# A two-layer trunk step: PSUM columns in one run over two banks, and taps of the up convolution read from PSUM

## The chip, the cores and the metric

The kernel runs on one core of one Trainium2 chip. The metric is the device time of one execution in microseconds, the median of three executions. One profiled execution, with a time of its own, gives the trace from which every row below is copied.

## What is computed

A trunk of two layers works on 128 prompt tokens and 512 sample tokens with 1024 channels. Each layer has a token-mixing half (attention, a convolution, a spatial gating and a pooling branch, gated and merged) and a gated feed-forward half. The second half, which the change touches most, is

```
def conv_ffn(h, lp):
    up = depthwise_conv(h @ lp['ffn_up'], lp['ffn_dw'], lp['ffn_dw_b'])
    gate, val = up[..., :D_FF], up[..., D_FF:]
    return (jax.nn.silu(gate) * val) @ lp['ffn_down']
```

with `D_FF = 2816` and a convolution of three taps along the tokens, padded with zeros at both ends of each group. All of it is float32 at the inputs and outputs.

## The kernel before, in words

**Layout.** Channels lie on the 128 partitions and tokens along the free dimension. A line has `TOK = 644` columns: 128 prompt tokens, two zero columns, 512 sample tokens, two zero columns. PSUM has eight banks of 512 float32 columns. The kernel uses them as four sets (0 to 3) of two banks, and a tile of 644 columns lies in a set as two halves of `HALF = 322`, one in each bank.

**Products.** Each large product is made in three float32r passes: the weights and the activations are both split in a high and a low part, and `hi*hi`, `lo*hi` and `hi*lo` are summed in PSUM (`product`, `first_group`, `down_chunk`). GpSimd splits the weights (`w_raw` into `w_hi` and `w_lo`, L435 and L437), 128x512 at a time, in a ring of four slots. So one output tile and one chunk of 128 input channels is three passes of two matmuls of 322 columns: three pairs. In a layer come the input projection (p1, 16 tiles), attention, the merge (`merge`, 8 steps), the output projection (`out`, 8 tiles), and then `up` (44 tiles of 8 chunks) and `down` (8 tiles of 22 chunks). Between the products stand RMS norms, in which TensorE does little.

**The up stage.** Its 44 tiles go in 11 steps of four, tile j of a step in PSUM set j. A step makes two pairs q: tiles 0 and 1 (gate and value of one chunk of 128 channels) and tiles 2 and 3. The first step is `first_group`, which runs over the input chunks outside and the tiles inside; the others run tile after tile. For each tile ScalarE (ACT) copies the 644 columns from PSUM into `up_x` in SBUF (L1157) and then gives the set free (L1159). For each pair VectorE (DVE) makes the middle tap with the bias out of `up_x` (L1666, two instructions), then the two outer taps (L1671, four instructions) into `up_y`; ScalarE takes the tanh (L1164); VectorE makes the gate and the product (L1678, L1681) into `act`.

**The ada work.** In steps 1 to 8 VectorE also sums three tiles of the modulation weights (`ada`, L1258 and L1260: 16 instructions of 384 columns) ahead of the pairs of that step. TensorE adds these sums over the partitions with twelve small matmuls (L528; six in the program, each of which stands in the trace as two) before tile 3 of the same step, into columns of tile 3's own set, and ScalarE keeps the result ahead of its copy of tile 3. So in a step TensorE waits before tile 3 for VectorE's sums; VectorE waits for tile 3 to be complete before pair 1, and the next sums stand behind pair 1 on its engine.

**The down stage.** Each chunk of `act` is split by ScalarE (`hi_part`, L1175) and VectorE (`lo_part`, L1688) and multiplied into all four sets (`down_chunk`, L838).

What sets the order is the order of the code on each engine, with counting semaphores between the engines: `set_full` and `set_empty` for the PSUM sets, `w_split` and `w_used` for the ring, `up_copied`, `up_conv`, `up_tanh`, `act_ready`.

Of the kernel before, what the change touches and what calls it, by code (L numbers as in the profile page):

```python
# [56 lines left out]
HALF = TOK // 2  # L57
# [81 lines left out]
EDGE = 8  # L139
# [7 lines left out]
def trunk_kernel(nc, x_in, cond_in, w_ada, w_lin, w_merge, w_pair, params_in, tables_in, ctx_ckv, ctx_kpe, const_in,  # L147
                 y_out, ckv_out, kpe_out):
    with ExitStack() as ctx:
# [95 lines left out]
        up_x = u("up_x", 0, 4 * 648, shape=[4, 648])  # L245
# [12 lines left out]
        def halves(s, lo=0, hi=P):  # L258

            return ps[lo:hi, 2 * s:2 * s + 2, 0:HALF]  # L260

# [7 lines left out]

        def two(ap):  # L270
            return ap.rearrange("p (a b) -> p a b", a=2)
# [203 lines left out]
        def _(pe):  # L475
# [4 lines left out]
            def product(L, phase, r, s, blocks, rhs, k_wait=None):  # L480
# [22 lines left out]
            def first_group(L, phase, rhs, k_wait):  # L503


                for k in range(DC):
# [4 lines left out]
                    for s in range(4):  # L511
                        whi, wlo = w_hi[:, k % SLOTS, s * P:(s + 1) * P], w_lo[:, k % SLOTS, s * P:(s + 1) * P]
                        for i, (w, a) in enumerate(((whi, hi), (whi, lo), (wlo, hi))):
                            for j in range(2):
                                last = pe.matmul(ps[:, 2 * s + j, 0:HALF], w, a[:, j * HALF:(j + 1) * HALF],  # L515
                                                 start=(k == 0 and i == 0), stop=(k == DC - 1 and i == 2))
# [5 lines left out]
            def ada(n, s):  # L522

                pe.wait_ge(ada_summed, n)
                for t in range(ADA_TRIO):
                    for g in range(2):
                        at = HALF + 2 * t + g
                        pe.matmul(ps[:, 2 * s, at:at + 1], ada_part[:, g, t, :], ones[:, 0:1], start=True, stop=True)  # L528
# [59 lines left out]
            with pe.Fori(0, DEPTH) as L:  # L588
# [154 lines left out]
                for c in range(2):  # L743
# [3 lines left out]
                    for j in range(2):  # L747
                        last = pe.matmul(ps[:, 2 * (2 + c) + j, 0:HALF], w, br[:, 8 + c, j * HALF:(j + 1) * HALF], start=True, stop=True)
# [78 lines left out]
                def down_chunk(pass_, chunk, nth, slot, par_, start, stop):  # L827
# [3 lines left out]
                    for s in range(4):  # L831
# [4 lines left out]
                        for i, (w, a) in enumerate(((whi, hi), (whi, lo), (wlo, hi))):  # L836
                            for j in range(2):
                                last = pe.matmul(ps[:, 2 * s + j, 0:HALF], w, a[:, j * HALF:(j + 1) * HALF],  # L838
                                                 start=(start and i == 0), stop=(stop and i == 2))
# [19 lines left out]
        def _(ac):  # L859
# [49 lines left out]
            def keep_ada(s, dst, t=0, n=ADA_TRIO):  # L909

                at = HALF + 2 * t
                return ac.activation(dst.rearrange("p a b -> p (a b)"), ps[:, 2 * s, at:at + 2 * n], ACT.Copy)
# [11 lines left out]
            with ac.Fori(0, DEPTH) as L:  # L924
# [41 lines left out]
                for c in range(2):  # L966
# [9 lines left out]
                    p0, in_first = 2 * EDGE + SEQ, HALF - SAMPLE0  # L976
# [894 lines left out]
```

## Time and profile before

| | us |
|---|---|
| median of three executions | 2735.32 (2733.73 to 2735.55) |
| the profiled execution | 2733.34 |
| its span in the trace | 2731.5 |
| TensorE matmul busy in it | 2473.2 |
| TensorE weight load busy | 2303.1 |
| VectorE busy | 1636.3 |
| ScalarE busy | 536.3 |
| GpSimd busy | 1303.7 |
| mean granted TensorE clock | 0.936 of 2.4 GHz |

Busy time of an engine is the union of its instructions. A matmul is drawn from its start until its result is through, and successive matmuls overlap, so the price of one in a stream is read from the distance of two starts, not from its duration. A "<-" in brackets names what ended an idle time.

### The profile page before, as it was taken

The page shows a single profiled execution, that of the slowest core. Times are in us where ns is not written, and L with a number is a line of the kernel's source. Part 1 is how long each engine was busy: PE and PEld are TensorE (multiplying, and loading weights), DVE is VectorE, ACT ScalarE, POOL GpSimd, SP SyncE. Part 2 cuts the span into 40 slices and gives each one's busy share as a digit, 9 for nine tenths or more (in the row PEclk, how much of TensorE's full clock was granted, in tenths as well). Part 3 has the DMA queues.
Part 4 walks back from the last instruction along what each step waited for, and adds up shares of the span by engine and source line. Part 5 has one row for each costly group of instructions (what it writes and reads, how often), then busy time and mean ns, then how long its engine had stood idle before and what let it go on. Part 6 is the DMA issues. An engine that isn't in the chain of part 4 may idle for free.

```text
span 2731.5 us, 44570 instructions
## 1 busy us (share of the span) xinstructions
PE 2473.2 (91%) x15092; PEld 2303.1 (84%) x15092; DVE 1636.3 (60%) x2288; ACT 536.3 (20%) x917; POOL 1303.7 (48%) x1232
## 2 busy tenths in 40 slices
PE   7897889999978999999969888899999789999996
PEld 7894449999977998899969745699999688889995
DVE  4558756444347777765473786644451677776655
ACT  1203432110022111112221144311011211111221
POOL 1458304555534544465525761165555244445552
PEclk9998989999978999999969989999999799999998
DMA  5110103333312333222212101133332133332221
GB/s 209 57 53 13 40 8 103 117 117 97 95 43 74 104 106 102 81 72 73 66 30 85 34 10 38 39 121 117 94 114 79 28 105 104 104 103 68 72 70 58
DMA packets 100479, 211.92 MB, mean 78 GB/s; under 512 B 10208, under 2 KB 17824, under 8 KB 100384
## 3 DMA queue, kind: packets, MB, share of 16 engines
q1 hardware_dynamic: 84832, 151.66, 18.9%
q10 hardware_dynamic: 15552, 59.02, 6.0%
q8 instruction: 57, 0.93, 0.1%
q14 instruction: 38, 0.31, 0.0%
HBM read 207.71 MB, written 2.93 MB: 77 GB/s over the span
## 4 chain that ended last, share of the span: by engine, by line
PE 68%; DVE 12%; DVEq 11%; ACT 3%; issue 3%; DMA 1%; ACTq 1%; SPq 0%
PE ps L495 37%; PE ps L838 10%; PE ps L515 6%; DVEq L1263 4%; DVE ada_part L1260 4%; PE ps L713 3%; PE ps L565 3%; DVEq L1668 2%; PE ps L528 2%; PE ps L659 1%; DVEq L1674 1%; DVEq L1529 1%; PE ps L689 1%; PE ps L702 1%; PE ps L579 1%
## 5 line engine op out<-in xcount | busy, mean ns | idle before, releaser
L435 POOL TENSOR_SCALAR w_hi<-w_raw 128x512 fp32r<-128x512 f32 x552 | 371.8, 674 | 1222.0 <-PE ps L495 296.4
L437 POOL TENSOR_TENSOR w_lo<-w_raw,w_hi 128x512 fp32r<-128x512 f32 x552 | 758.7, 1374 | 81.4 <-issue 1.2
L495 PE MATMUL ps<-h_hi,w_hi 128*128 128x322 f32 x2688 | 636.5, 319 | 0.0
L495 PE MATMUL ps<-h_lo,w_hi 128*128 128x322 f32 x2688 | 631.9, 317 | 0.0
L495 PE MATMUL ps<-h_hi,w_lo 128*128 128x322 f32 x2688 | 627.8, 315 | 0.0
L495 PEld LDWEIGHTS ps<-h_lo,w_hi 128*128 128x128 f32 x2688 | 466.9, 194 | 0.0
L495 PEld LDWEIGHTS ps<-h_hi,w_hi 128*128 128x128 f32 x2688 | 465.2, 194 | 1.3 <-issue 1.3
L495 PEld LDWEIGHTS ps<-h_hi,w_lo 128*128 128x128 f32 x2688 | 466.1, 194 | 0.0
L1260 DVE SCALAR_TENSOR_TENSOR ada_part<-ada_raw,cond,ada_part 128x384 f32<-128x384 f32 x448 | 341.5, 803 | 19.3 <-issue 3.4
L1688 DVE TENSOR_TENSOR a_lo<-act,a_hi 128x644 fp32r<-128x644 f32 x88 | 135.3, 1541 | 148.6 <-ACT a_hi L1175 147.6
L1671 DVE SCALAR_TENSOR_TENSOR up_y<-up_x,par,up_y 128x644 f32<-128x644 f32 x176 | 179.3, 1060 | 13.2 <-issue 11.3
L838 PE MATMUL ps<-a_hi,w_hi 128*128 128x322 f32 x704 | 162.8, 313 | 6.7 <-DVE a_lo L1688 6.7
L838 PE MATMUL ps<-a_hi,w_lo 128*128 128x322 f32 x704 | 163.1, 313 | 0.0
L838 PE MATMUL ps<-a_lo,w_hi 128*128 128x322 f32 x704 | 162.8, 312 | 0.0
L1617 DVE SCALAR_TENSOR_TENSOR mtmp<-gate_t,ps 128x644 f32<-128x644 f32 x48 | 39.4, 821 | 173.0 <-ACT gate_t L1106 114.7
L1666 DVE TENSOR_SCALAR up_y<-up_x,par 128x644 f32<-128x644 f32 x88 | 65.1, 782 | 123.1 <-ACT up_x L1157 123.1
L838 PEld LDWEIGHTS ps<-a_hi,w_hi 128*128 128x128 f32 x704 | 119.6, 191 | 8.0 <-DVE a_lo L1688 7.8
L838 PEld LDWEIGHTS ps<-a_hi,w_lo 128*128 128x128 f32 x704 | 119.6, 191 | 0.0
L838 PEld LDWEIGHTS ps<-a_lo,w_hi 128*128 128x128 f32 x704 | 119.5, 191 | 0.0
L1106 ACT ACTIVATE gate_t<-ps,half_gate 128x644 f32<-128x644 f32 x64 | 51.3, 801 | 340.6 <-PE ps L495 337.2
L1223 DVE TENSOR_TENSOR sq_sum<-sq_sum,sq 128x644 f32<-128x644 f32 x38 | 39.3, 1035 | 128.5 <-ACT sq L867 127.0
L1164 ACT ACTIVATE up_t<-up_y 128x644 f32<-128x644 f32 x44 | 32.7, 744 | 414.3 <-DVE up_y L1671 414.3
(200 smaller groups left out, 3492.4 us busy)
## 6 DMA issues: line engine op xcount, KB each, us to landing
w_raw<-in_w_lin_dram SPq DMA_DIRECT2D x360, 256.0 KB, 2.6
ada_raw<-in_w_ada_dram ACTq DMA_DIRECT2D x32, 1536.0 KB, 6.7
w_raw<-in_w_merge_dram SPq DMA_DIRECT2D x144, 256.0 KB, 2.7
ada_pre<-in_w_ada_dram ACTq DMA_DIRECT2D x4, 2048.0 KB, 21.8
w_raw<-in_w_merge_dram SPq DMA_DIRECT2D x48, 128.0 KB, 2.0
pw<-in_w_pair_dram SPq DMA_DIRECT2D x8, 640.0 KB, 3.9
x<-in_x_dram SPq DMA_DIRECT2D x8, 322.0 KB, 6.0
out_y_dram<-x SPq DMA_DIRECT2D x8, 322.0 KB, 2.3
```

The costliest lines, as they stand in the source:

```text
L435: pool.tensor_scalar(w_hi[:, s, 0:n * P], raw, 1.0, 0.0, ALU.mult, ALU.add)
L437: pool.tensor_tensor(w_lo[:, s, 0:n * P], raw, w_hi[:, s, 0:n * P], ALU.subtract).then_inc(w_split[s], 1)
L495: last = pe.matmul(ps[:, 2 * s + j, 0:HALF], w, a[:, j * HALF:(j + 1) * HALF], start=(k == 0 and i == 0), stop=(k == total - 1 and i == 2))
L515: last = pe.matmul(ps[:, 2 * s + j, 0:HALF], w, a[:, j * HALF:(j + 1) * HALF], start=(k == 0 and i == 0), stop=(k == DC - 1 and i == 2))
L565: last = pe.matmul(ps[:, 6, b:b + 1], sq[:, c % 2, BLOCK_COL[b]:BLOCK_COL[b] + P], ones[:, 0:1], start=False, stop=(c == DC - 1 and b == N ...
L713: pe.matmul(ps[0:V_HEAD, 7, :], v_pair[:, b, vs], probs_t[:, b, :], start=(b == 0), stop=(b == 4))
L838: last = pe.matmul(ps[:, 2 * s + j, 0:HALF], w, a[:, j * HALF:(j + 1) * HALF], start=(start and i == 0), stop=(stop and i == 2))
L1260: last = dv.scalar_tensor_tensor(out=acc[:, g, 0:n, :], in0=w, scalar=cond[:, k, g:g + 1], in1=acc[:, g, 0:n, :], op0=ALU.mult, op1=ALU.add)
L1263: dv.drain()
L1666: dv.tensor_scalar(up_y[:, j, :], up_x[:, j, 2:2 + TOK], col("ffn_dw", v, 1), col("ffn_dw_b", v), ALU.mult, ALU.add)
L1671: last = dv.scalar_tensor_tensor(out=up_y[:, j, :], in0=up_x[:, j, 1 + tap:1 + tap + TOK], scalar=col("ffn_dw", v, tap), in1=up_y[:, j, :] ...
L1688: dv.tensor_tensor(a_lo[:, n % 2, :], src, a_hi[:, n % 2, :], ALU.subtract).then_inc(a_ready, 1)
```

## The change

The 644 columns of a tile lie in one run: columns 0 to 511 fill the first bank of the set, columns 512 to 643 the first 132 columns of the second. Each pass of a product is now three matmuls, of 256, 256 and 132 columns. The first opens the accumulation in the first bank, the second ends it; the third does both in the second bank. The ada columns move behind column 132 of the second bank. Every reader of a tile takes 644 columns in one run instead of two halves, at the same count; only the pooling input needs one copy less (2 for 3 of them, four times in all).

In the up stage ScalarE's copy to `up_x` becomes the middle tap itself: an activation `Identity` with the tap as scale and the bias, out of PSUM into `up_y`. VectorE's two instructions of the middle tap are gone; its four outer taps read 643 columns straight from PSUM, where neighbouring tokens lie side by side. The set is given free by VectorE after its taps and no longer by ScalarE after its copy. `up_x` and its zeroed edges are gone, and ScalarE's middle tap waits for `act_ready` of the step before, since `up_y` is written earlier.

```
-HALF = TOK // 2
+BANK = 512
+REST = TOK - BANK
+PARTS = ((0, 0, 256, True, False), (0, 256, 256, False, True), (1, 0, REST, True, True))
...
         def halves(s, lo=0, hi=P):
 
-            return ps[lo:hi, 2 * s:2 * s + 2, 0:HALF]
+            return line(s, TOK, lo, hi)
...
+        def par_col(name, i, j, tap=0):
+
+            at = PCOL[name] + tap * 2 * FFC + j
+            return par[:, i * 4 + at:i * 4 + at + 1] if isinstance(i, int) else par[:, bass.ds(i * 4 + at, 1)]
...
                         for i, (w, a) in enumerate(((whi, hi), (whi, lo), (wlo, hi))):
-                            for j in range(2):
-                                last = pe.matmul(ps[:, 2 * s + j, 0:HALF], w, a[:, j * HALF:(j + 1) * HALF],
-                                                 start=(k == 0 and i == 0), stop=(k == total - 1 and i == 2))
+                            for bank, at, m, opens, ends in PARTS:
+                                col = bank * BANK + at
+                                last = pe.matmul(ps[:, 2 * s + bank, at:at + m], w, a[:, col:col + m],
+                                                 start=(k == 0 and i == 0 and opens), stop=(k == total - 1 and i == 2 and ends))
...
-                        if j % 2 == 0:
-
-                            ac.wait_ge(up_conv, L * FFC + (q + 1) + i * 2)
-                        ac.activation(two(up_x[:, j, 2:2 + TOK]), halves(j), ACT.Copy).then_inc(up_copied, 1)
-                        ac.wait_ge(up_copied, L * (2 * FFC) + (j + 1) + i * 4)
-                        ac.sem_inc(set_empty[j], 1)
+                        if j % 2 == 0 and not first:
+
+                            ac.wait_ge(act_ready, L * FFC + q + i * 2 - 1)
+                        ac.activation(up_y[:, j, :], halves(j), ACT.Identity, scale=par_col("ffn_dw", i, j, 1), bias=par_col("ffn_dw_b", i, j))\
+                            .then_inc(up_copied, 1)
...
                         dv.wait_ge(up_copied, L * (2 * FFC) + (2 * q + 2) + i * 4)
-                        for v in range(2):
-                            j = 2 * q + v
-                            dv.tensor_scalar(up_y[:, j, :], up_x[:, j, 2:2 + TOK], col("ffn_dw", v, 1), col("ffn_dw_b", v), ALU.mult, ALU.add)
-                        for tap in (0, 2):
-                            dv.drain()
+                        for tap, of, to in ((0, 0, 1), (2, 1, 0)):
                             for v in range(2):
                                 j = 2 * q + v
-                                last = dv.scalar_tensor_tensor(out=up_y[:, j, :], in0=up_x[:, j, 1 + tap:1 + tap + TOK], scalar=col("ffn_dw", v, tap),
-                                                               in1=up_y[:, j, :], op0=ALU.mult, op1=ALU.add)
+                                dst = up_y[:, j, to:to + TOK - 1]
+                                last = dv.scalar_tensor_tensor(out=dst, in0=line(j, TOK)[:, of:of + TOK - 1], scalar=par_col("ffn_dw", i, j, tap),
+                                                               in1=dst, op0=ALU.mult, op1=ALU.add)
+                            if tap == 0:
+                                dv.drain()
                         last.then_inc(up_conv, 1)
                         dv.drain()
+                        for v in range(2):
+                            dv.sem_inc(set_empty[2 * q + v], 1)
```

`first_group` and `down_chunk` get the same `PARTS` loop as `product`.

On TensorE, in the loop over steps 1 to 8 of the up stage, at the ada matmuls and the start of tile 3 (`ps` is PSUM, `h_hi` and `h_lo` the activations, `w_hi` and `w_lo` the weights), before:

```order
1197 L816 REGISTER_ALU
1198 L524 REGISTER_ALU
1199 L528 MATMUL ps<-const,ada_part 128x1 x6
1200 L495 MATMUL ps<-h_hi,w_hi 128x322 x2
1201 L495 MATMUL ps<-h_lo,w_hi 128x322 x2
1202 L495 MATMUL ps<-h_hi,w_lo 128x322 x2
```

and with the change:

```order
2069 L824 REGISTER_ALU
2070 L532 REGISTER_ALU
2071 L536 MATMUL ps<-const,ada_part 128x1 x6
2072 L502 MATMUL ps<-h_hi,w_hi 128x256 x2
2073 L502 MATMUL ps<-h_hi,w_hi 128x132
2074 L502 MATMUL ps<-h_lo,w_hi 128x256 x2
2075 L502 MATMUL ps<-h_lo,w_hi 128x132
2076 L502 MATMUL ps<-h_hi,w_lo 128x256 x2
2077 L502 MATMUL ps<-h_hi,w_lo 128x132
```

Each pass of two matmuls has become one of three; nothing else moved there. On ScalarE, in the same loop, from tile 0 to tile 2, before:

```order
412 L1156 ISA [waits set_full0]
413 L1157 ACTIVATE up_x<-ps 128x644 [waits up_conv]
414 L1158 ISA
415 L1140 REGISTER_ALU [waits up_copied]
416 L1157 ACTIVATE up_x<-ps 128x644 [waits set_full1]
417 L1158 REGISTER_ALU
418 L1163 REGISTER_ALU [waits up_copied]
419 L1164 ACTIVATE up_t<-up_y 128x644 [waits up_conv]
420 L1140 REGISTER_ALU
421 L1156 REGISTER_ALU [waits set_full2]
422 L1157 ACTIVATE up_x<-ps 128x644 [waits up_conv]
```

and with the change:

```order
400 L1164 ISA [waits set_full0]
401 L1165 ISA [waits act_ready]
402 L1165 REGISTER_ALU
403 L1165 ACTIVATE up_y<-ps,par 128x644
404 L1148 REGISTER_ALU
405 L1165 ISA [waits set_full1]
406 L1165 ACTIVATE up_y<-ps,par 128x644
407 L1170 REGISTER_ALU
408 L1171 ACTIVATE up_t<-up_y 128x644 [waits up_conv]
409 L1148 REGISTER_ALU
410 L1164 REGISTER_ALU [waits set_full2]
411 L1165 ISA [waits act_ready]
```

The activation out of PSUM stays, with the tap and the bias from `par`; its wait for `up_copied` and the release behind it are gone, and `act_ready` stands where `up_conv` stood. On VectorE, one pair of a step without ada work, before:

```order
607 L1666 TENSOR_SCALAR up_y<-up_x,par 128x644 [waits up_copied]
608 L1666 TENSOR_SCALAR up_y<-up_x,par 128x644
609 L1671 SCALAR_TENSOR_TENSOR up_y<-up_x,par,up_y 128x644 x4
610 L1677 REGISTER_ALU
611 L1678 SCALAR_TENSOR_TENSOR up_t<-up_t,up_y 128x644 [waits up_tanh]
612 L1681 SCALAR_TENSOR_TENSOR act<-up_t,up_y 128x644
```

and with the change:

```order
589 L1667 SCALAR_TENSOR_TENSOR up_y<-ps,par,up_y 128x643 [waits up_copied]
590 L1667 SCALAR_TENSOR_TENSOR up_y<-ps,par,up_y 128x643 x3
591 L1677 REGISTER_ALU
592 L1678 SCALAR_TENSOR_TENSOR up_t<-up_t,up_y 128x644 [waits up_tanh]
593 L1681 SCALAR_TENSOR_TENSOR act<-up_t,up_y 128x644
```

The two instructions of the middle tap are gone and the four outer taps read `ps` instead of `up_x`.

## Rows read from the trace of the kernel before

**Rows 1.** The page, part 1: busy us (share of the span) xinstructions.

```profile
PE 2473.2 (91%) x15092; PEld 2303.1 (84%) x15092; DVE 1636.3 (60%) x2288; ACT 536.3 (20%) x917; POOL 1303.7 (48%) x1232
```

**Rows 2.** Groups on PE, shapes apart: xcount | busy us, mean ns | idle before.

```profile
L495 PE MATMUL ps<-h_hi,w_hi 128*128 128x322 f32 x2688 | 636.5, 319 | 0.0
L838 PE MATMUL ps<-a_hi,w_hi 128*128 128x322 f32 x704 | 162.8, 313 | 6.7 <-DVE a_lo L1688 6.7
...
L495 PE MATMUL ps<-br_hi,w_hi 128*128 128x322 f32 x320 | 73.3, 310 | 0.0
...
L515 PE MATMUL ps<-h_hi,w_hi 128*128 128x322 f32 x256 | 62.9, 329 | 16.0 <-DVE h_lo L1325 16.0
...
L515 PE MATMUL ps<-mg_hi,w_hi 128*128 128x322 f32 x128 | 29.8, 314 | 2.4 <-DVE mtmp L1617 2.4
...
L495 PE MATMUL ps<-mg_hi,w_hi 128*128 128x322 f32 x128 | 29.5, 312 | 0.0
...
L641 PE MATMUL ps<-ws_t,tok_major 128*64 128x128 f32 x80 | 4.8, 275 | 3.7 <-DVEq L1480 3.7
```

**Rows 3.** Timeline of PE in p1 of the second layer: start us, us, what, xcount.

```profile
1480.24 0.46 PE L495 MATMUL ps<-h_hi,w_hi 128*128 128x322 f32 x2
...
1489.77 0.46 PE L495 MATMUL ps<-h_hi,w_lo 128*128 128x322 f32 x2
```

**Rows 4.** Windows: us, PE busy (x), PEld, DVE, ACT, POOL, PEclk, DMA share, GB/s.

```profile
1300.00:1360.00 60.00, 60.00 (x406) 60.00 (x405) 26.95 (x17) 12.66 (x17) 33.09 (x32) 1.00 0.26 75
```

**Rows 5.** Timeline of the weight loads, attention's matmuls of 512, 256 and 128 columns.

```profile
216.80 0.19 PEld L668 LDWEIGHTS ps<-ckv,pw 128*128 128x128 f32 x1 [0.24 <-issue]
217.23 0.62 PEld L668 LDWEIGHTS ps<-ckv,pw 128*128 128x128 f32 x3 [0.24 <-issue]
217.88 2.86 PEld L676 LDWEIGHTS ps<-pw,ckv 128*128 128x128 f32 x24
```

**Rows 6.** Timeline of the weight loads: ada matmuls of one column, then 322.

```profile
443.87 1.42 PEld L528 LDWEIGHTS ps<-const,ada_part 128*128 128x128 f32 x12 [1.01 <-DVE ada_part L1260]
445.20 0.30 PEld L495 LDWEIGHTS ps<-h_hi,w_hi 128*128 128x128 f32 x2
```

**Rows 7.** Windows of the up stage: layer 0, one step of it, layer 1.

```profile
878.00:1136.50 258.50, 227.76 (x1431) 225.61 (x1429) 202.30 (x237) 29.25 (x50) 125.53 (x115) 0.92 0.32 102
...
920.40:955.30 34.90, 31.74 (x206) 31.47 (x205) 27.72 (x33) 4.17 (x7) 17.68 (x16) 0.95 0.31 105
...
2212.40:2471.00 258.60, 227.90 (x1431) 225.75 (x1429) 202.28 (x237) 29.24 (x50) 125.53 (x115) 0.92 0.32 102
```

**Rows 8.** Timeline of PE: the waits for the ada sums in layer 0.

```profile
886.98 2.72 PE L528 MATMUL ps<-const,ada_part 128*128 128x1 f32 x12 [8.67 <-DVE ada_part L1260]
...
958.79 2.05 PE L528 MATMUL ps<-const,ada_part 128*128 128x1 f32 x12 [3.16 <-DVE ada_part L1260]
```

**Rows 9.** Timeline of DVE, one step: pair 1, then the next ada sums.

```profile
935.95 1.37 DVE L1666 TENSOR_SCALAR up_y<-up_x,par 128x644 f32<-128x644 f32 x2 [3.84 <-ACT up_x L1157]
937.50 2.04 DVE L1671 SCALAR_TENSOR_TENSOR up_y<-up_x,par,up_y 128x644 f32<-128x644 f32 x2 [0.18 <-issue]
...
958.66 0.61 DVE L1666 TENSOR_SCALAR up_y<-up_x,par 128x644 f32<-128x644 f32 x1
```

**Rows 10.** Groups on DVE with a PSUM operand or of the up stage.

```profile
L1671 DVE SCALAR_TENSOR_TENSOR up_y<-up_x,par,up_y 128x644 f32<-128x644 f32 x176 | 179.3, 1060 | 13.2 <-issue 11.3
...
L1617 DVE SCALAR_TENSOR_TENSOR mtmp<-gate_t,ps 128x644 f32<-128x644 f32 x48 | 39.4, 821 | 173.0 <-ACT gate_t L1106 114.7 <-PE ps L495 57.6 <-issue 0.8
```

**Rows 11.** Timelines at the end of the first up step: DVE, PE.

```profile
855.89 1.14 DVE L1666 TENSOR_SCALAR up_y<-up_x,par 128x644 f32<-128x644 f32 x2 [11.59 <-ACT up_x L1157]
...
856.66 0.46 PE L495 MATMUL ps<-h_hi,w_hi 128*128 128x322 f32 x2
```

**Rows 12.** Timelines at the start of the down stage: ACT, PE.

```profile
1205.80 0.71 ACT L1157 ACTIVATE up_x<-ps 128x644 f32<-128x644 f32 x1 [3.82 <-PE ps L495]
...
1214.65 0.57 PE L838 MATMUL ps<-a_hi,w_hi 128*128 128x322 f32 x2 [1.85 <-DVE a_lo L1688]
```

More of the change, by code:

```diff
@@ L513, in first_group @@
                         for i, (w, a) in enumerate(((whi, hi), (whi, lo), (wlo, hi))):
-                            for j in range(2):
-                                last = pe.matmul(ps[:, 2 * s + j, 0:HALF], w, a[:, j * HALF:(j + 1) * HALF],
-                                                 start=(k == 0 and i == 0), stop=(k == DC - 1 and i == 2))
+                            for bank, at, m, opens, ends in PARTS:
+                                col = bank * BANK + at
+                                last = pe.matmul(ps[:, 2 * s + bank, at:at + m], w, a[:, col:col + m],
+                                                 start=(k == 0 and i == 0 and opens), stop=(k == DC - 1 and i == 2 and ends))
                         if k == DC - 1:
@@ L526, in ada @@
                     for g in range(2):
-                        at = HALF + 2 * t + g
-                        pe.matmul(ps[:, 2 * s, at:at + 1], ada_part[:, g, t, :], ones[:, 0:1], start=True, stop=True)
+                        at = REST + 2 * t + g
+                        pe.matmul(ps[:, 2 * s + 1, at:at + 1], ada_part[:, g, t, :], ones[:, 0:1], start=True, stop=True)
             def two_blocks(j):
@@ L746, in _ @@
                     w = tables[:, 768 + c * P:768 + (c + 1) * P]
-                    for j in range(2):
-                        last = pe.matmul(ps[:, 2 * (2 + c) + j, 0:HALF], w, br[:, 8 + c, j * HALF:(j + 1) * HALF], start=True, stop=True)
+                    for bank, n in ((0, BANK), (1, REST)):
+                        last = pe.matmul(ps[:, 2 * (2 + c) + bank, 0:n], w, br[:, 8 + c, bank * BANK:bank * BANK + n], start=True, stop=True)
                     last.then_inc(set_full[2 + c], 1)
@@ L836, in down_chunk @@
                         for i, (w, a) in enumerate(((whi, hi), (whi, lo), (wlo, hi))):
-                            for j in range(2):
-                                last = pe.matmul(ps[:, 2 * s + j, 0:HALF], w, a[:, j * HALF:(j + 1) * HALF],
-                                                 start=(start and i == 0), stop=(stop and i == 2))
+                            for bank, at, m, opens, ends in PARTS:
+                                col = bank * BANK + at
+                                last = pe.matmul(ps[:, 2 * s + bank, at:at + m], w, a[:, col:col + m],
+                                                 start=(start and i == 0 and opens), stop=(stop and i == 2 and ends))
                         if stop:
@@ L909, in keep_ada @@
             def keep_ada(s, dst, t=0, n=ADA_TRIO):
-                at = HALF + 2 * t
-                return ac.activation(dst.rearrange("p a b -> p (a b)"), ps[:, 2 * s, at:at + 2 * n], ACT.Copy)
+                at = REST + 2 * t
+                return ac.activation(dst.rearrange("p a b -> p (a b)"), ps[:, 2 * s + 1, at:at + 2 * n], ACT.Copy)
             for i in range(ADA_LOADS):
@@ L975, in _ @@
                     ac.wait_ge(pool_x_free, L * 3 + (c + 1))
[L976 removed]
+                    p0 = 2 * EDGE + SEQ
                     ac.activation(pool_x[:, EDGE:EDGE + SEQ], ps[:, 2 * s, 0:SEQ], ACT.Copy)
[L978 to L979 removed]
+                    ac.activation(pool_x[:, p0:p0 + DEC_SEQ], line(s, TOK)[:, SAMPLE0:SAMPLE0 + DEC_SEQ], ACT.Copy)\
                         .then_inc(set_empty[s], 1)
@@ L1645, in _ @@
                 next_h(L, "gap2", L * 2 + 1, L * NINV + 3, mods(L, ADA_TRIOS), MOD_FFN, ADA, "pre_ffn_g")
-                for j in range(4):
-                    dv.memset(up_x[:, j, 0:2], 0.0)
-                    dv.memset(up_x[:, j, 2 + TOK:4 + TOK], 0.0)
-                dv.drain()
                 def up_step(i, last_step=False, with_ada=False):
@@ L1655, in up_step @@
                     for q in range(2):
-                        def col(name, v, tap=0):
-                            at = PCOL[name] + tap * 2 * FFC + 2 * q + v
-                            return par[:, i * 4 + at:i * 4 + at + 1] if isinstance(i, int) else par[:, bass.ds(i * 4 + at, 1)]
                         if last_step and q == 1:
```

9 lines of the change are left out of this document (2 added, 7 removed).

## The prediction

> **What bounds the kernel now.** I read the engines' busy shares first: TensorE's matmuls fill 91% of the span and VectorE 60% [rows 1]. Then TensorE's groups: six groups of float32r matmuls of 322 columns, with 2688, 704, 320, 256, 128 and 128 instructions, and each has two companions of the same count for the other passes [rows 2]. That is 3 x 4224 = 12,672 matmuls, or 6336 pairs, and their idle time before is small. In p1 two rows that stand 32 rows (64 matmuls) apart start 9.53 us apart, so one matmul costs 148.9 ns and a pair 297.8 ns [rows 3]; a window of the down stage agrees, 406 in 60 us without a gap, at the full clock of 2.4 GHz [rows 4]. 6336 x 0.2978 = 1887 us: the kernel is for two thirds of its time a stream of these pairs.
>
> One place is different, the up stage with ada work. From the first wait for the sums to the end of the eighth it takes 258.5 us in layer 0 and 258.6 in layer 1, seven steps plus one wait [rows 7]. TensorE waits there 8.67 us once and then 3.16 us in each step for VectorE's ada sums [rows 8], and the mean clock is 0.92, because after each wait it is granted 1.2 GHz for a while. Its own work at full clock is 96 pairs and twelve one-column matmuls, 28.6 + 1.3 = 29.9 us, against steps of 34.9 us [rows 7]. So here VectorE's and TensorE's hand-over bounds.
>
> **The change, part by part.**
>
> *Three matmuls for two.* Each pass keeps its 644 columns but loads its weights three times instead of twice: 6336 more matmuls and weight loads. What does one cost? The 148.9 ns of 322 columns are 134.2 ns of columns at 2.4 GHz and 14.7 ns more. For 256 columns that gives 118.4 ns if the surplus goes with the columns and 121.4 ns if it is fixed. For 132 columns the columns alone would be 61 ns, but the next weights must be loaded meanwhile. Twelve matmuls of one column, which have nothing but their loads to do, take 1.33 us until the next, 111 ns each, and the first float32r load behind them, drawn with its successor as 0.30 us of which the last load is 0.19, also takes 0.11 us [rows 5, 6]. So the 132-column part costs a weight load, 111 ns. The triple is 2 x 118.4 + 111 = 348 or 2 x 121.4 + 111 = 354 ns; I take **351 ns**, 53.2 ns over a pair. From below it can't be under three weight loads, 3 x 111 = 333 ns. From above a 256-column part can't cost more than a 322-column one, 2 x 148.9 + 111 = 409; but the float32 rows of attention go with their columns, 0.43 us for 512, (0.62 - 0.19)/2 = 0.215 for 256 and (2.86 - 0.19)/23 = 0.116 for 128 at two cycles a column [rows 5], so I put the working upper end at three times the fixed surplus, 3 x 121.4 = 364 ns, and leave more to a rival.
>
> The Trainium skill, TensorE: Matmul & The Clock Gate, section LDWEIGHTS (loading the stationary operand), gives a load of 128 columns as 128/1.2, 107 ns, so it too says that a 132-column matmul doesn't hide the next load; the trace has 111. The same page's section Back-to-back issue gap has a rule against this: N/2.4 + 2.5 ns for a lone matmul, 109 + 109 + 57.5 = 276 ns for a triple. By that rule a pair would be 273 ns, where the trace has 298.
>
> *Where this lies on the path.* Of the 6336 pairs 2 x 7 x 96 = 1344 lie in the two stretches of the up stage above. The other 4992 run where TensorE waits for next to nothing: 4992 x 0.0532 = **+265.6 us**. Only a wait before the spatial gating's matmuls, 3.7 us in all for VectorE [rows 2], is filled by the longer stream: **-3.7 us**.
>
> *The up stage with ada.* TensorE's step becomes 96 x 0.351 + 1.33 = 35.0 us. VectorE's cycle before was: sums ready at 923.8 (the next are ready at 958.66, one step of 34.9 later), then ada matmuls, tile 3 and ScalarE's copy until 935.95, then 1.55 us for the middle tap, then 21.16 us for the outer taps, the gate and the next sums [rows 7, 9]. The middle tap leaves VectorE (ScalarE's activation stays as one of 0.7 us); tile 3 grows by 24 x 0.0532 = 1.3 us. That is 12.15 + 1.3 + 21.16 = 34.6 us, and some 2 us less once tile 3 is no longer run at the half clock. Both are under 35.0: TensorE becomes the bound, its waits of 8.67 and 3.16 us go, and with them the half clock. Seven steps: 245.2 us for 258.5, **-26.7 us** over both layers. With 333 ns the step is 33.3 and with 364 ns 36.3 us, -51 and -9 us.
>
> *Taps from PSUM.* An instruction of the same kind with one PSUM operand takes 821 ns in the merge, where those of `up_x` take 1060 on average [rows 10]. I leave this gain at nothing: VectorE is hidden behind TensorE now. It would be worth something only if VectorE bounded again.
>
> *Sets given free later.* ScalarE released a set after its copy; VectorE now does after the taps of the pair. In a running step this is hidden: pair 0's taps, some 3.5 us, start when the sums are ready, and TensorE then has the ada matmuls and tile 3, 9.8 us, before it wants set 0. It shows twice in a layer. After `first_group` all four tiles end together: VectorE starts at 855.89 and TensorE goes on at 856.66 [rows 11]; the taps now end 3.5 us after such a start, so TensorE waits about 2.6 us. What is late next is nothing: its ada sums are then ready before tile 3. At the start of the down stage sets 2 and 3 come free about 4.8 us after the last up tile, where TensorE wants set 2 after 2.1 us: 2.6 us, of which the present wait of 1.85 us for `a_lo` two chunks later [rows 12] is given back. 2 x (2.6 + 0.7) = **+6.6 us**. Bounds: 0 if the waits overlap others, 12 if the next wait stays. The ada columns' new place, the pooling copy and the dropped zeroing cost nothing I can see; ScalarE, 20% busy, covers them.
>
> *The sum.* 2733.3 (the profiled execution) + 265.6 - 3.7 - 26.7 + 6.6 = 2975.1. The median of the runs is 2.0 above the profiled one: **2977 us**, 8.8% slower.
>
> **The rivals.**
>
> A. *A short float32r matmul costs more than its columns or its load.* No row shows one under 322 columns. If the 132-column part fell to the float32 price (attention's matmuls of 128 columns are two records of 111 ns each), it would cost 223: the triple is 461 ns, the 4992 pairs 815 us, and seven steps of 45.6 us 319 us for 258.5, +121: about 3675. If every float32r matmul cost 149 ns whatever its width (a price per instruction), the triple is 447 ns: 745 + 101 us, about 3585. For it: the surplus of 14.7 ns over the columns is unexplained, where the float32 matmuls have 2 to 5. Against it: one load behind one-column matmuls took 0.11 us [rows 6], and float32 matmuls, issued just like these, go at 111.
>
> B. *Faster: the loads hide.* If the second and third load of the same weights cost nothing and only columns count, a triple stays at 298 ns and only the up stage moves: VectorE's cycle, with tile 3 at 7.1 us and full clock, is 8.5 + 1.8 + 21.2 = 31.5 us (1.8 is an estimate for the copy of 0.7 [rows 12] with its hand-overs), 220 us for 258.5 in each layer, -76: 2733.3 - 76 + 6.6 + 2 = 2666. The point from which it decides: with the stage still bound by VectorE, at (76 - 7)/4992 = 14 ns more for a triple, or 312 ns, gain and loss are even. Against it: today both halves load the same weights and each load is there, 15,092 for 15,092 matmuls [rows 1], and one-column matmuls still take 111 ns. By the skill's lone-matmul rule above the estimate would be 4992 x -0.022 more, about 2556.
>
> C. *VectorE stays the bound in the up stage.* If the taps from PSUM took 1.7 us each instead of 0.8 (VectorE and TensorE on PSUM at once), its cycle gains 4 x 0.8 us and is 36 us: +14 us, 2991. For it: nothing in the trace reads PSUM at such a rate beside matmuls; against it the merge's 821 ns, taken beside a full TensorE [rows 10].
>
> That the change doesn't do what it says is out: the order of the changed kernel has the three matmuls.
>
> **How the numbers follow.** Forecast 0.78, A 0.12, B 0.05, C 0.05. With the bounds of the triple: 333 ns gives 2733 + 176 - 51 + 5 = 2863, 364 ns gives 2733 + 330 - 9 + 5 = 3059; the uncertain waits add 6. I give **2870 to 3070**, since the lower end needs every surplus gone; C lies inside, A and B outside with 0.17. Faster by over 0.2% (about what a measurement of this kernel can tell from no change): 0.04, B. Within 0.2%: 0.01. Slower: 0.95.
>
> **What would show it.** In the changed trace: 19,008 float32r matmuls; starts 118 to 121 ns apart for the 256s and 111 from the 132 to the next; eight merge steps longer by 126 x 53 ns = 6.7 us each; in the up stage no wait before the ada matmuls, steps of 35.0 us and a full clock; TensorE waits of 2 to 3 us after `first_group` of `up` and at the start of `down`, for VectorE. A is shown by starts of over 140 ns behind the short part, B by ones near 61. I am wrong as a whole if TensorE stays below the full clock in a stream that is load-bound for a third of its matmuls.

## The result, and the profile after

| | before | after |
|---|---|---|
| median of the runs beside each other, us | 2734.53 (2732.31 to 2735.55) | 2943.53 (2940.08 to 2944.98) |
| ratio, 95% interval | | 1.0764 [1.0745, 1.0782] |
| the profiled execution, us | 2733.34 | 2940.08 |
| its span, us | 2731.5 | 2938.3 |
| mean granted TensorE clock | 0.936 | 0.958 |

The changed kernel is 7.6% slower: 206.7 us between the two profiled executions, where the prediction's sum had 241.8. One of the 13 executions of the kernel before that were timed beside the run of 322s with the copy (below) took 4735 us at a granted clock of 1.0; it stands in no ratio here. The engines' busy times and the chain that ended last, from the page of after (the first line answers to [rows 1]):

```profile
PE 2742.8 (93%) x21428; PEld 2581.0 (88%) x21428; DVE 1520.9 (52%) x2184; ACT 554.0 (19%) x913; POOL 1265.9 (43%) x1232
...
PE 87%; DVE 5%; DVEq 2%; ACT 2%; issue 2%; DMA 1%; ACTq 0%; SPq 0%
```

TensorE has 21428 - 15092 = 6336 matmuls more and holds 87% of the chain that ended last; in the same line of the page of before it was 68%, with 12% for VectorE and 11% for its sequencer. The kernel has become more purely a TensorE kernel, at a better clock, and slower.

Groups of after, shapes apart (columns as in [rows 2]; the VectorE line answers to [rows 10]):

```profile
L502 PE MATMUL ps<-h_hi,w_hi 128*128 128x256 f32 x2688 | 605.1, 306 | 5.1 <-DVEq L1672 5.1
...
L502 PE MATMUL ps<-h_hi,w_hi 128*128 128x132 f32 x1344 | 302.7, 225 | 0.0
...
L847 PE MATMUL ps<-a_hi,w_hi 128*128 128x256 f32 x704 | 157.8, 306 | 5.5 <-DVEq L1672 5.0 <-DVE a_lo L1688 0.5
...
L649 PE MATMUL ps<-ws_t,tok_major 128*64 128x128 f32 x80 | 4.8, 275 | 0.0
```

```profile
L1667 DVE SCALAR_TENSOR_TENSOR up_y<-ps,par,up_y 128x643 f32<-128x643 f32 x176 | 147.8, 881 | 247.0 <-ACT up_y L1165 240.7 <-issue 5.4
```

The only new waits of TensorE are those for `L1672`, the release of the sets behind VectorE's taps: once in `up` and once in `down` in each layer, 2.5 us each. The wait of 3.7 us before the spatial gating is gone. A tap out of PSUM takes 881 ns, one out of `up_x` took 1060.

The stream itself, in p1 of the second layer, three matmuls a row (answers to [rows 3]):

```profile
1553.50 0.51 PE L523 MATMUL ps<-h_hi,w_lo 128*128 128x256 f32 x3
...
1559.41 0.51 PE L502 MATMUL ps<-h_lo,w_hi 128*128 128x256 f32 x3
```

The second row stands 17 rows below the first (where `first_group`, L523, has given way to `product`, L502), 5.91 us later: a pass of 256 + 256 + 132 takes 347.6 ns. The 216 passes between the eighth ada matmuls and `down` agree: 75.09 us, 347.6 ns each. The pair of before took 297.8.

Windows of after: a piece of the down stage, the up stage from the first ada matmul to the eighth in layer 0 and in layer 1, and from the end of `first_group` to the first ada matmul (columns as in [rows 4]; the middle two answer to [rows 7] without its first wait):

```profile
1400.00:1460.00 60.00, 60.00 (x521) 60.00 (x520) 24.29 (x14) 10.40 (x14) 28.13 (x29) 1.00 0.21 62
...
966.40:1209.30 242.90, 242.90 (x2103) 242.90 (x2102) 164.20 (x196) 35.46 (x50) 114.03 (x112) 1.00 0.33 106
...
2403.50:2646.30 242.80, 242.80 (x2102) 242.80 (x2101) 164.26 (x196) 35.35 (x50) 114.00 (x112) 1.00 0.33 106
...
937.30:966.40 29.10, 26.57 (x216) 26.58 (x217) 26.20 (x31) 5.05 (x7) 13.09 (x12) 0.94 0.33 108
```

In the up stage TensorE has no gap in 242.9 us, at the full clock: seven steps of 34.7 us. Before, the same seven steps took 249.5 us; with the wait ahead of them they are the 258.5 us of [rows 7], at a clock of 0.92. The three starts that matter, in the timeline of TensorE of after (the first answers to [rows 11], the second to [rows 8], the third to [rows 12]):

```profile
939.83 0.56 PE L502 MATMUL ps<-h_hi,w_hi 128*128 128x256 f32 x3 [2.53 <-DVEq L1672]
...
966.45 1.45 PE L536 MATMUL ps<-const,ada_part 128*128 128x1 f32 x12
...
1290.45 0.56 PE L847 MATMUL ps<-a_hi,w_hi 128*128 128x256 f32 x3 [2.50 <-DVEq L1672]
```

The ada matmuls no longer wait; the two new waits stand where sets are wanted that VectorE has just read.

Where the 206.7 us came from, by stages (us, from the start of the first matmul of each):

| stage | before, layer 0 / 1 | after | difference | predicted, each layer |
|---|---|---|---|---|
| p1 | 128.3 / 127.1 | 144.3 / 144.2 | +16.0 / +17.1 | +18.6 |
| attention | 205.3 / 207.3 | 204.1 / 204.0 | -1.2 / -3.3 | 0 |
| merge | 312.7 / 312.5 | 362.3 / 362.3 | +49.6 / +49.8 | +53.6 |
| out | 59.4 / 59.4 | 69.0 / 69.0 | +9.6 / +9.6 | +10.2 |
| up to its first ada matmul | 60.6 / 60.6 | 65.4 / 65.4 | +4.8 / +4.8 | -1.8 with the next |
| first to eighth ada matmul | 249.5 / 249.6 | 242.9 / 242.9 | -6.6 / -6.7 | |
| eighth ada matmul to down | 69.0 / 69.0 | 76.4 / 76.4 | +7.4 / +7.4 | +11.5 |
| down | 165.6 / 165.2 | 189.1 / 189.0 | +23.5 / +23.8 | +28.8 |

The last column is the prediction's sum spread over the stages: 384, 1008, 192, 168 + 672, 216 and 528 passes in a layer, with its waits and, for the up stage, its seven steps. The norms inside the layers are the same to 0.1 us; the norm between the layers takes 0.6 us more, the start 0.7 and the tail 0.2.

### The profile page after: what moved, and what is told of

It is laid out like the page before. It is cut to its first block, busy times and chain, and to the rows that moved or that the text cites. A ratio compares the mean times of both kernels' runs of the same rounds, so it can differ in the third digit from the quotient of the medians.

```text
span 2938.3 us, 56947 instructions
## 1 busy us (share of the span) xinstructions
PE 2742.8 (93%) x21428; PEld 2581.0 (88%) x21428; DVE 1520.9 (52%) x2184; ACT 554.0 (19%) x913; POOL 1265.9 (43%) x1232
## 4 chain that ended last, share of the span: by engine, by line
PE 87%; DVE 5%; DVEq 2%; ACT 2%; issue 2%; DMA 1%; ACTq 0%; SPq 0%
PE ps L502 56%; PE ps L847 12%; PE ps L523 7%; PE ps L721 3%; PE ps L573 2%; PE ps L536 1%; PE ps L667 1%; DVEq L1535 1%; PE ps L697 1%; PE ps L710 1%; PE ps L587 1%; DMA ada_pre<-in_w_ada_dram 1%; ACT probs L1021 1%; DVE conv_acc L1550 1%; PE ps L684 1%
## 5 line engine op out<-in xcount | busy, mean ns | idle before, releaser
L502 PE MATMUL ps<-h_hi,w_hi 128*128 128x256 f32 (+1 forms) x4032 | 688.6, 279 | 5.1 <-DVEq L1672 5.1
L502 PE MATMUL ps<-h_hi,w_lo 128*128 128x256 f32 (+1 forms) x4032 | 687.0, 279 | 0.0
L502 PE MATMUL ps<-h_lo,w_hi 128*128 128x256 f32 (+1 forms) x4032 | 686.5, 279 | 0.0
L502 PEld LDWEIGHTS ps<-h_hi,w_hi 128*128 128x128 f32 x4032 | 561.8, 189 | 6.7 <-issue 6.7
L502 PEld LDWEIGHTS ps<-h_lo,w_hi 128*128 128x128 f32 x4032 | 562.7, 190 | 0.0
L502 PEld LDWEIGHTS ps<-h_hi,w_lo 128*128 128x128 f32 x4032 | 562.3, 189 | 0.0
L1267 DVE SCALAR_TENSOR_TENSOR ada_part<-ada_raw,cond,ada_part 128x384 f32<-128x384 f32 x448 | 346.6, 814 | 17.1
L1667 DVE SCALAR_TENSOR_TENSOR up_y<-ps,par,up_y 128x643 f32<-128x643 f32 x176 | 147.8, 881 | 247.0 <-ACT up_y L1165 240.7
L847 PE MATMUL ps<-a_hi,w_hi 128*128 128x256 f32 (+1 forms) x1056 | 179.5, 278 | 5.5 <-DVEq L1672 5.0
L847 PE MATMUL ps<-a_hi,w_lo 128*128 128x256 f32 (+1 forms) x1056 | 179.6, 278 | 0.0
L847 PE MATMUL ps<-a_lo,w_hi 128*128 128x256 f32 (+1 forms) x1056 | 178.9, 277 | 0.0
```

Of the source, the lines that this page charges most:

```text
L502: last = pe.matmul(ps[:, 2 * s + bank, at:at + m], w, a[:, col:col + m], start=(k == 0 and i == 0 and opens), stop=(k == total - 1 and i = ...
L847: last = pe.matmul(ps[:, 2 * s + bank, at:at + m], w, a[:, col:col + m], start=(start and i == 0 and opens), stop=(stop and i == 2 and ends))
L1267: last = dv.scalar_tensor_tensor(out=acc[:, g, 0:n, :], in0=w, scalar=cond[:, k, g:g + 1], in1=acc[:, g, 0:n, :], op0=ALU.mult, op1=ALU.add)
L1667: last = dv.scalar_tensor_tensor(out=dst, in0=line(j, TOK)[:, of:of + TOK - 1], scalar=par_col("ffn_dw", i, j, tap), in1=dst, op0=ALU.mult ...
```

## The experiments

Theory: a float32r matmul costs its columns or one weight load of 111 ns, whichever is longer, and a pass is the sum of its parts. The taps read from PSUM free TensorE from its waits in the up stage. Rivals: each matmul has a price of its own whatever its width; repeated loads of the same weights are free; the layout (a run over two banks) costs something in its readers.

In the kernels below the changed kernel's parts come from two numbers, with the matmul loops otherwise as they are: `START`, the first column of the run in its set, and the sizes of the parts. Every reader takes the run from `START` on.

**The load for itself: two parts, 512 and 132.**

```
-PARTS: 256, 256, 132 from column 0
+PARTS: 512, 132 from column 0
```

> The changed kernel with two matmuls a pass instead of three: 512 columns fill the first bank, 132 the second. Theory (a part costs its columns at 0.462 ns each or the next weight load of 111 ns, whichever is longer): 512 x 0.462 + 111 = 348 ns for 644 columns, as in the changed kernel, so its time stays at 2935 to 2950 us although a third of the matmuls is gone. Rival 1 (the third matmul costs some 50 ns as an instruction): the pass falls back to 298 ns and the kernel to about 2680 us. Rival 2 (each load adds its share to the columns it lies beside): two loads instead of three give about 315 ns, some 2780 us.

Measured: 2914.59 us (2913.61 to 2919.46), ratio 1.0667 [1.0649, 1.0685]. Timeline of TensorE in p1, two matmuls a row:

```profile
1544.83 0.51 PE L508 MATMUL ps<-h_hi,w_hi 128*128 128x512 f32 x2
...
1551.69 0.50 PE L508 MATMUL ps<-h_hi,w_lo 128*128 128x512 f32 x2
```

Twenty rows, 6.86 us: 343 ns a pass. With as many matmuls and loads as before (15,092), the kernel is 6.7% slower, since one part of the two is under a load's time; the kernel of the next experiment, which differs from it in the two sizes and the first column alone, is 253 us faster. So it isn't the number of instructions: what costs is a part too short to cover the load of the next weights. The measured time lies 20 us below the theory's range. The 512-column matmul must then be 343 - 111 = 232 ns, 18.7 over its 213.3 of columns, where the theory had let the surplus grow with the columns.

**The taps alone: 322 and 322, in one run.**

```
-PARTS: 256, 256, 132 from column 0
+PARTS: 322, 322 from column 190
```

> The changed kernel with the run of 644 columns begun at column 190 of a set, so that 322 columns lie in each bank and a pass is two matmuls of 322 again; taps from PSUM stay. It is the second part of the change alone. Theory: TensorE's stream is that of before (298 ns a pair), and in the up stage VectorE bounds with a step of 31.5 to 33 us for 35.6, with waits of some 2.7 us at two places of each layer: 2665 to 2700 us, faster than both kernels. Rival (reading the taps from PSUM or giving the sets free later costs something in each step): 2735 us or more.

Measured: 2661.72 us (2659.44 to 2663.43), ratio 0.9738 [0.9722, 0.9755]: the only kernel here that beats both, by 72 us under before and 282 under after, and 3 us below the expected range. The window from the first to the eighth ada matmul, then one wait of TensorE for the sums, then VectorE's taps, in layer 0:

```profile
887.00:1106.30 219.30, 214.63 (x1429) 212.76 (x1429) 168.16 (x197) 35.74 (x50) 118.27 (x112) 0.98 0.36 118
...
917.86 1.50 PE L541 MATMUL ps<-const,ada_part 128*128 128x1 f32 x12 [0.67 <-DVE ada_part L1271]
...
930.47 1.68 DVE L1671 SCALAR_TENSOR_TENSOR up_y<-ps,par,up_y 128x643 f32<-128x643 f32 x2 [5.75 <-ACT up_y L1169]
```

31.3 us a step, where before has 35.6 between these two marks; rival B had worked out 31.5 from VectorE's cycle. The wait for the sums shrinks from 3.16 us [rows 8] to 0.67, and the clock rises from 0.92 to 0.98. The seven steps of both layers give 60.7 us, the pieces of the up stage before and behind them another 13.9. p1, merge, out and the norms don't move.

**The triple alone: parts as in the changed kernel, the up stage with its copy.**

The copy's waits and `up_x` with its zeroed edges come back too; of the edit this is the core (`...` marks cuts, within lines too):

```
-ac.activation(up_y[:, j, :], halves(j), ACT.Identity, scale=..., bias=...)
+ac.activation(two(up_x[:, j, 2:2 + TOK]), halves(j), ACT.Copy)
+ac.sem_inc(set_empty[j], 1)
...
+dv.tensor_scalar(up_y[:, j, :], up_x[:, j, 2:2 + TOK], ...)   # middle tap, two of them
-in0=line(j, TOK)[:, of:of + TOK - 1]                           # outer taps
+in0=up_x[:, j, 1 + tap:1 + tap + TOK]
```

> The first part of the change alone: one run over two banks in parts of 256, 256 and 132, but ScalarE copies to SBUF, VectorE makes all three taps from there and ScalarE gives the set free, as before. Theory: the stream costs 348 ns a pass, +250 us, and in the up stage TensorE's 34.7 us and VectorE's 34 to 35.5 us nearly tie, so the taps' part is worth little under the triple: 2945 to 2965 us. Rival (the later release costs more than the taps save): under 2940 us.

Measured: 2961.09 us (2959.01 to 2961.74), ratio 1.0832 [1.0814, 1.085]. The same seven steps, and one start of the ada matmuls:

```profile
965.90:1218.30 252.40, 251.30 (x2101) 250.25 (x2101) 197.75 (x225) 29.25 (x50) 124.19 (x112) 0.97 0.30 101
...
965.93 2.72 PE L537 MATMUL ps<-const,ada_part 128*128 128x1 f32 x12 [4.78 <-DVE ada_part L1269]
```

252.4 us against the 242.9 with the taps from PSUM. The longer stream alone already fills most of the waits: the first one, ahead of this window, is 4.78 us for 8.67, and within it TensorE is idle for 1.1 us. What stays is the clock of 0.97.

**The layout alone: 322 and 322 in one run, with the copy.** This kernel has the parts of `e2` and the up stage of `e3`.

> The kernel before with nothing changed but the layout: the 644 columns lie in one run over the two banks, begun at column 190, in two matmuls of 322; ScalarE copies to SBUF and VectorE takes its taps from there. Theory (a run over two banks costs and gives nothing by itself; all that the run of 322s with taps from PSUM gained comes from the taps' part): within 0.2% of before, 2727 to 2738 us. Rival (half of that gain is the layout's): under 2705 us.

Measured: 2733.72 us (2731.04 to 2735.96, ten runs), ratio 1.0001 [0.9992, 1.0011]. A run that begins in the middle of a bank and goes on in the next costs its readers nothing: ScalarE's copy of a tile takes 701 ns in either kernel. The four kernels together, medians in us:

| | taps from `up_x` | taps from PSUM | gain |
|---|---|---|---|
| 322 + 322 | 2733.7 | 2661.7 | 72.0 |
| 256 + 256 + 132 | 2961.1 | 2943.5 | 17.6 |
| loss | 227.4 | 281.8 | |

The two parts of the change are not a sum of two numbers: where the stream is longer, TensorE's waits are largely filled already, and the taps have little left to give.

**Three parts of nearly the same size: 214, 214, 216.**

```
-PARTS: 256, 256, 132 from column 0
+PARTS: 214, 214, 216 from column 84
```

> The changed kernel with three even parts: 214, 214 and 216 columns (the run begins at column 84 of a set). Theory: each part has less than 111 ns of columns, so each costs one load: 3 x 111 = 333 ns for 348, which is 75 us off the stream and 19 us off the fourteen up steps: 2840 to 2870 us. Rival 1 (a price per instruction) and rival 2 (a share per load): no change, 2943 us. Rival 3 (float32r parts under 256 columns are slow by themselves): slower than 2960 us, since all three are short now.

Measured: 2871.62 us (2871.03 to 2872.58), ratio 1.0504 [1.0487, 1.0522]; once more beside another kernel (below) 2872.03.

```profile
1500.03 0.50 PE L528 MATMUL ps<-h_lo,w_hi 128*128 128x214 f32 x3
...
1505.73 0.49 PE L528 MATMUL ps<-h_hi,w_hi 128*128 128x214 f32 x3
```

Seventeen rows, 5.70 us: 335 ns a pass, three parts of 111 to 113 ns, 72 us less than the changed kernel with as many matmuls. The range was missed by 2 us. Here every part is at the load's price, which gives the theory's second case directly, and shows what the changed kernel's division loses: 256 columns are over the load's time, 132 far under it, and the excess of one doesn't pay for the lack of the other.

**An uneven triple: 322, 162, 160.**

```
-PARTS: 256, 256, 132 from column 0
+PARTS: 322, 162, 160 from column 190
```

> The changed kernel with three matmuls a pass, of 322, 162 and 160 columns (the run begins at column 190). Theory: 149 + 111 + 111 = 372 ns a pass for 348, as two parts are short now and one is longer than a load: +24 ns on 6336 passes, about 3095 us. Rival (three matmuls cost the same whatever their sizes): 2943 us.

Measured: 3102.37 us, in one execution.

```profile
1649.91 0.54 PE L508 MATMUL ps<-h_lo,w_hi 128*128 128x322 f32 x3
...
1652.89 0.54 PE L508 MATMUL ps<-h_hi,w_hi 128*128 128x322 f32 x3
```

Eight rows, 2.98 us: 372.5 ns a pass, against 149 + 111 + 111 = 371. With the same number of matmuls as the changed kernel it is 159 us slower, so a price for each matmul whatever its width falls: three divisions of the same 644 columns in three matmuls give 335, 348 and 373 ns. That the 111 ns are the load's is read from the matmuls of one column [rows 6]; no run changes the size of the load in this stream, so it isn't shown apart. A floor of 111 ns under every matmul they are not: the gating's 80 matmuls, whose weights have 64 columns, take 4.8 us in all, 60 ns each on average [rows 2].

**Four parts: 162, 160, 162, 160.**

```
-PARTS: 256, 256, 132 from column 0
+PARTS: 162, 160, 162, 160 from column 190
```

> The changed kernel with four matmuls a pass, of 162, 160, 162 and 160 columns (the run begins at column 190 of a set). Theory (a part costs its columns or one weight load of 111 to 112 ns, whichever is longer): 4 x 112 = 447 ns for 348, 99 ns more on each of 6336 passes: about 3570 us. Rival (the fourth matmul adds only the 12 to 15 ns that stand over the columns): about 2943 + 90 = 3035 us.

Measured: 5814.7 us in one execution, at a mean granted clock of 0.587. Both the theory and the rival missed by more than 2000 us, so the kernel was run again, four times, with the even triple as a control beside it.

> The kernel with four matmuls a pass (162, 160, 162, 160 columns) once more, timed in rounds beside the kernel before: its one run took 5815 us with a granted clock of 0.587, at 1.2 GHz from 434 us of the span on for most of the time, though TensorE was busy 97%. Theory 1 (the stream of short parts itself lets the chip grant only 1.2 GHz): every run takes 5700 to 5900 us with a clock near 0.59, while the kernel before stays at 2734 us and 0.936. Theory 2 (that one run was disturbed by something outside the kernel): about 3570 us with a clock over 0.9.

> The three even parts of 214, 214 and 216 columns once more beside it, as the control on the same chip: 2865 to 2880 us with a clock near 0.954, if load-bound parts alone don't lower the clock.

Measured: 5866.78 us (5816.82 to 5869.51), ratio 2.1399 [2.1296, 2.1503], with the kernel before at 2734.27 and the even triple at 2872.03 beside it. The text on record for this run puts the fall of the clock at 434 us of the span; that is wrong: the first trace has the long fall from 727.6 us on, the second from 665.4. From the page of the second trace: its busy times, and the granted clock in 40 slices, in tenths of full speed; then two windows in the merge and the whole first long stretch (columns as in [rows 4]):

```profile
PE 5678.8 (97%) x27764; PEld 5515.9 (94%) x27764; DVE 1447.4 (25%) x2184; ACT 557.5 (10%) x913; POOL 1221.2 (21%) x1232
...
PEclk9999755555555555555556996555555555555555
```

```profile
600.00:640.00 40.00, 40.00 (x360) 40.00 (x360) 8.27 (x9) 3.31 (x5) 14.34 (x17) 1.00 0.26 86
...
800.00:860.00 60.00, 60.00 (x283) 60.00 (x282) 15.67 (x22) 2.34 (x3) 12.20 (x14) 0.50 0.13 41
...
665.40:3191.30 2525.90, 2485.56 (x11605) 2476.98 (x11604) 491.52 (x699) 178.28 (x263) 464.64 (x488) 0.50 0.11 34
```

In the first window the law holds: 360 parts in 40 us, 111 ns each. In the second TensorE is as busy, without a gap, but is granted 0.50, and a part takes 212 ns. Nothing is waited for there; the same stream of instructions runs at 1.2 GHz, for 2526 us on end, and from 3566.7 us on, in the merge of the second layer, for 2298 us more. It is this kernel that brings it, in all five of its executions on two occasions: the kernels run beside it on the second were where they always are.

What TensorE did just before the fall is the same each time. Its timeline of the second trace, one pass a row:

```profile
663.48 0.61 PE L508 MATMUL ps<-br_hi,w_lo 128*128 128x162 f32 x4
663.93 1.43 PE L541 MATMUL ps<-const,ada_part 128*128 128x1 f32 x12
665.22 0.99 PE L508 MATMUL ps<-h_hi,w_hi 128*128 128x162 f32 x4
666.01 1.05 PE L508 MATMUL ps<-h_lo,w_hi 128*128 128x162 f32 x4
```

A pass takes 0.45 us above and 0.85 below. The clock falls at 665.4, just behind the twelve one-column ada matmuls, which had no wait before them. All four long stretches of the two traces begin so (at 727.6 and 3516.2 us in the first, 665.4 and 3566.7 in the second); the ada matmuls one or two merge steps earlier, at the same full clock, brought no fall. The other kernels know the beginning too: wherever one of them lost the clock in a stream without gaps, it was behind the twenty one-column matmuls in p1. In the kernel before, layer 0:

```profile
140.32 1.17 PE L539 MATMUL ps<-const,sq_sum 128*128 128x1 f32 x10
141.35 1.25 PE L539 MATMUL ps<-const,sq_sum_kv 128*128 128x1 f32 x10
...
144.25 0.74 PE L495 MATMUL ps<-h_hi,w_lo 128*128 128x322 f32 x2
```

But there, as in every other division of the columns, the full clock came back after 3.4 to 6.8 us. In the stream of 160 and 162 columns it stayed away until p1 of the second layer, where it came back at 3191.3 us (3140.8 in the first trace), among four float32 matmuls of 512 columns; pairs of such matmuls had passed four times before without bringing it back. So the runs show where the clock is lost and in which stream it doesn't return. Why it doesn't isn't settled: no run has this stream without the one-column matmuls.

The Trainium skill, TensorE: Matmul & The Clock Gate, section Loop structure matters more than you think, has it that dense matmuls, one behind the other, keep the clock up. The traces agree only in part: in this kernel a stream without gaps was held at 1.2 GHz for thousands of us, in the others it had the full clock but for the few us behind one-column matmuls.

## Why the prediction held, and where its terms were off

**The cost of a short part held.** The 132-column part was taken as a weight load of 111 ns, from twelve one-column matmuls and the one load behind them [rows 5, 6]. The even triple measures this price directly (335 ns for three), and 322 + 162 + 160 agrees (372.5 for 371). Rival A falls with them: no short part came near 149 or 223 ns at the full clock. Rival B's first half falls with `e1`, which has the number of matmuls and loads of the kernel with two 322s and takes 343 ns a pass, where the rival needed 298.

**The size of the triple was 3.4 ns too high**: 347.6 measured, 351 taken as the middle between 348 (surplus with the columns) and 354 (fixed surplus). With 6336 passes that is 21.5 us of the 35.1 by which the sum was over. The lower end was the right one: 347.6 - 111 = 2 x 118.3, 11.6 over the columns of a 256, is the surplus in proportion to the columns (11.7). For 512 columns proportion would give 23.4 and the runs have 18.7, so neither form is right over the whole range.

**VectorE gave up the bound in the up stage, as said.** 34.7 us a step for 35.0 predicted; it is 96 x 0.3476 + 1.33 = 34.7, TensorE's own work and nothing else. VectorE now waits for TensorE. Rival C is out: the taps took 881 ns, where it needed 1700, and the kernel with 322-column pairs, where VectorE still bounds, took 31.3 us a step.

**The two new waits were sized right, what follows one of them was not.** 2.53 and 2.50 us for 2.6. But behind the first one the clock falls, in after's timeline of TensorE (one pass a row):

```profile
940.57 0.51 PE L502 MATMUL ps<-h_hi,w_lo 128*128 128x256 f32 x3
940.92 0.74 PE L502 MATMUL ps<-h_hi,w_hi 128*128 128x256 f32 x3
941.46 0.84 PE L502 MATMUL ps<-h_lo,w_hi 128*128 128x256 f32 x3
942.10 0.84 PE L502 MATMUL ps<-h_hi,w_lo 128*128 128x256 f32 x3
```

Starts 0.35 us apart become 0.64 apart. The clock of 0.94 over 29.1 us (the last of the windows above) is 1.7 us, where before had 1.00 in the same place; with a `first_group` at 0.92 for 0.94, another 1.1, the up stage lost 2.8 us in a layer that the prediction didn't have. It came out at -1.8 to -1.9 us for -1.8 only because the shorter triple gave 2.9 us back. This agreement is a coincidence of two errors. Behind the wait at the start of `down` the clock stayed at 1.00; a wait of 2.5 us doesn't bring the fall every time.

**The half clock that went elsewhere was overlooked.** The prediction counted the return of the full clock up to the eighth wait for the sums only. Before's windows behind that wait and at the start of `down`, and the second wait for `a_lo` in that stage:

```profile
1136.50:1205.80 69.30, 69.28 (x446) 69.28 (x447) 46.85 (x42) 11.05 (x18) 40.85 (x36) 0.95 0.23 65
1205.80:1222.00 16.20, 14.35 (x87) 14.09 (x86) 11.95 (x11) 3.58 (x5) 8.91 (x8) 0.89 0.22 66
...
1292.86 0.57 PE L838 MATMUL ps<-a_hi,w_hi 128*128 128x322 f32 x2 [1.53 <-DVE a_lo L1688]
```

The clock of 0.95 over 69.3 us is 3.4 us, of 0.89 over 16.2 us 1.7 us, and the wait puts two starts 1.99 us apart that would be 0.30 apart, 1.7 us. After has 1.00 in both stretches and no such wait. So the 216 passes behind the eighth wait cost 216 x 0.0498 = 10.8 less 3.4, measured +7.4; the 528 of `down` 26.3 + 0.65 (a wait of 2.50 for one of 1.85) less 1.7 and 1.7, 23.5, measured 23.5 and 23.8. The step that failed is the count of what leaves with a wait: it ended the stretch at the last wait itself, not at the end of the half clock behind it.

**The sum again**, over both layers, against the predicted 241.8: triple -21.5; behind the eighth wait -6.7; down -6.6; clock behind the new wait and in `first_group` +5.6; p1 -1.5, most of it in layer 0, where before has the 3.4 us of half clock behind one-column matmuls shown above and after has none; merge -1.0; attention -4.5; start, tail and rests +1.3. That is 241.8 - 34.9 = 206.9, measured 206.7. The matmuls of attention weren't changed. Its 4.5 us are nearly all TensorE's busy time (171.1 to 168.7 us in layer 0, 169.3 to 167.4 in layer 1), at a clock up from 0.88 to 0.90 and from 0.89 to 0.91, and not its waits: those for VectorE's `probs` are 37.4 us for 36.3. In the traces of the experiments a layer's attention takes anything from 202 to 208 us, in no order that follows the change, so this term says nothing of it. The sum was right in sign and near in size, and nearly all terms erred to the same side.

**What would show it, checked.** 19,008 float32r matmuls: so. Merge steps of +6.7 us: 49.7/8 = 6.2. No wait before the ada matmuls and a full clock: so. Waits of 2 to 3 us at the two places: so. "Starts 118 to 121 ns apart for the 256s and 111 from the 132 to the next": not so. The trace shows 168 from one 256 to the next, 117.5 from the 256 to the 132, and 61.7 from the 132 to the next 256. Their sum is right, but the wait for the load is drawn one matmul later than I had it. By itself, the 61.7 would have been read as rival B. One has to add up a whole pass before deciding.

## To carry to other kernels

Divide the columns of a pass so that no part is shorter than a weight load: the cost of a pass is the sum over its parts of the longer of columns and load, and one part of 512 beside one of 132 is dearer than two of 322. A gain from a removed wait and a loss on the engine that waited don't add: the longer stream fills the wait first, so test the two halves of a change apart (here +227 and -72 us, together +209). When a wait goes or comes, count the time at half clock behind it as well, and end the count where the clock is back. Look at the granted clock when the parts get short: the four parts should have cost 30% over the kernel before and cost 114%.

## What the runs showed of the hardware

**A TensorE stream without gaps can run at half clock.** Parts of 160 and 162 columns, each at the price of a load, were granted 1.2 GHz for most of the run, from some one-column matmuls on: 5867 us instead of the 3570 that 447 ns a pass would give. Parts of 214 and 216, also at the load's price, kept 0.954. The prediction named a lower clock as what would make it wrong as a whole; it didn't come with this change, but it came with the next shorter parts.

**The wait for a load appears one matmul late** in the distances of starts: 61.7 ns behind a short part and 168 behind the one after it; 282 and 61 for 512 and 132; 186, 77 and 110 for 322, 162 and 160.

**The surplus of a float32r matmul over its columns** is 11.6 ns at 256 columns, 14.7 at 322 and 18.7 at 512, neither fixed nor in proportion. No run tells what it is. The Trainium skill, TensorE: Matmul & The Clock Gate, section Back-to-back issue gap, gives sustained figures of some 81 ns for 128 columns and 131 for 512. The traces don't agree for float32r: 111 ns for 132 columns and 232 for 512.

**ScalarE and VectorE read a tile over two banks without a price**, and VectorE's taps took less from PSUM (881 ns) than from SBUF (1060). ScalarE's activation with a scale and a bias for each partition takes 885 ns, where the plain copy took 0.71 us [rows 12].
